# Giving up the unread TensorE products of a two-block model kernel (attention, mixers, routers, experts) on one Trainium2 core

## What is computed

```python
for layer in range(DEPTH):                      # first block
    z = rmsnorm(x, norm_mix[layer]) @ w_in[layer]
    x = x + concatenate([o_a, o_b, o_c, o_d]) @ w_out[layer]
    h = rmsnorm(x, norm_ffn[layer])
    x = x + (silu(h @ w_gate[layer]) * (h @ w_up[layer])) @ w_down[layer]
for i in range(DEPTH):                          # second block
    y = conformer_conv(h, ...) if i == 0 else short_gated_conv(h, ...)
    x = layer_norm(ALPHA * x + (1.0 + g_m) * y, ...)
    y = hierarchical_moe(h, ...)                # group, two experts a token
    x = layer_norm(ALPHA * x + (1.0 + g_f) * y, ...)
```

## The kernel before

| place | code | where | products |
|---|---|---|---|
| A | `ahead_of_scores(8)`, line 896 | between `values(8)` and `scores(10)`, in each layer's attention | 2, twice |
| B | line 2562 | between `conformer_in` and `normed_back(0)` (transposes, line 2475), ahead of `mix_out` (line 2507) | 3 |
| C | lines 2586 and 2599 | behind the router's products (line 2536) and behind the five small counting products (lines 2594 to 2598), in each expert layer | 4 and 1, twice |
| D | line 2884 | at the end of the first expert layer, ahead of `tile_transposes` (line 2393) and `gated_in` (line 2492) | 2 |

## Time and profile before

### The profile page before, as it was taken

One profiled execution on the slowest core, in us unless ns is written; L12 is line 12 of the kernel. 1 busy time (PEld: TensorE's weight loads), 2 busy tenths in 40 slices (PEclk: granted clock), 3 DMA queues, 4 the chain that ended last, 5 costly groups with the idle time before them and its releaser, 6 DMA issues.

```text
span 1958.8 us, 20949 instructions
## 1 busy us (share of the span) xinstructions
PE 1859.0 (95%) x8122; PEld 944.4 (48%) x8122; DVE 852.5 (44%) x1556; ACT 342.2 (17%) x800; POOL 93.0 (5%) x137
## 2 busy tenths in 40 slices
PE   8999999999999999999999999989999988989887
PEld 4555665456556654855343433433875323323222
DVE  1576888834778988864112111112325101111102
ACT  2453111124531102122011100101002100000000
POOL 4102000001020001201000000000000000000000
PEclk9999999999999999999999999999999999999999
DMA  9315877752168876666999999999448999999996
GB/s 308 106 60 175 307 286 266 256 186 56 60 232 290 296 293 227 185 251 233 420 425 430 432 431 431 432 430 409 161 188 335 428 430 431 430 431 432 430 429 281
DMA packets 138028, 603.18 MB, mean 308 GB/s; under 512 B 15864, under 2 KB 59816, under 8 KB 122560
## 3 DMA queue, kind: packets, MB, share of 16 engines
q1 hardware_dynamic: 131904, 591.41, 76.3%
q0 software_dynamic: 5136, 10.25, 2.0%
q10 hardware_dynamic: 880, 0.07, 0.0%
HBM read 597.70 MB, written 1.10 MB: 306 GB/s over the span
## 4 chain that ended last, share of the span: by engine, by line
PE 67%; DMA 22%; DVE 6%; DVEq 2%; issue 1%; ACT 1%; SPq 1%; ACTq 0%
PE ps L2706 15%; DMA ring<-in_e_w_gate 14%; PE ps L955 13%; PE ps L657 7%; DMA ring<-in_e_w_up 7%; PE ps L1038 5%; PE ps L2492 4%; PE ps L2742 4%; PE ps L2422 3%; PE ps L2507 2%; PE ps L2627 2%; PE ps L756 2%; PE ps L2605 2%; DMA ring<-in_e_w_down 1%; DMA ring<-in_b_w_in 1%
## 5 line engine op out<-in xcount | busy, mean ns | idle before, releaser
L2706 PE MATMUL ps<-ring,hT 128*64 128x512 f32 (+1 forms) x960 | 218.9, 609 | 28.8 <-DMA ring<-in_e_w_gate 17.6
L2706 PE MATMUL ps<-ring,late 128*64 128x512 f32 (+1 forms) x880 | 203.1, 606 | 24.8 <-DMA ring<-in_e_w_gate 14.5
L2742 PE MATMUL ps<-ring,qkT 128*64 128x512 f32 (+1 forms) x960 | 205.6, 594 | 2.8 <-DMA ring<-in_e_w_down 2.7
L657 PE MATMUL ps<-ring,hT 128*128 128x512 f32 (+1 forms) x384 | 171.0, 589 | 0.0
L2706 PEld LDWEIGHTS ps<-ring,hT 128*64 128x64 f32 (+1 forms) x960 | 68.6, 126 | 173.9 <-issue 173.9
L3375 DVE TENSOR_TENSOR qkT<-ps,qkT 128x512 f32<-128x512 f32 (+1 forms) x32 | 22.1, 690 | 279.5 <-PE ps L2706 277.1
L3351 DVE TENSOR_TENSOR qkT<-ps,qkT 128x512 f32<-128x512 f32 (+1 forms) x64 | 44.2, 690 | 218.1 <-PE ps L2742 218.0
L2706 PEld LDWEIGHTS ps<-ring,late 128*64 128x64 f32 (+1 forms) x880 | 64.7, 126 | 153.4 <-issue 153.3
L1680 DVE SCALAR_TENSOR_TENSOR qkT<-ring,cc,qkT 128x512 f32<-128x512 f32 x168 | 125.8, 749 | 8.2
L2742 PEld LDWEIGHTS ps<-ring,qkT 128*64 128x64 f32 (+1 forms) x960 | 61.1, 123 | 129.0 <-issue 128.6
L3370 DVE TENSOR_TENSOR x<-ps,x 128x1024 f32<-128x1024 f32 x22 | 26.9, 1224 | 194.4 <-PE ps L2605 194.4
(11 more groups left out here) (480 smaller groups left out, 2316.6 us busy)
## 6 DMA issues: line engine op xcount, KB each, us to landing
ring<-in_e_w_down SPq DMA_DIRECT2D x26, 4096.0 KB, 21.1
ring<-in_e_w_gate SPq DMA_DIRECT2D x26, 4096.0 KB, 21.8
ring<-in_e_w_up SPq DMA_DIRECT2D x24, 4096.0 KB, 21.8
ring<-in_ada_w SPq DMA_DIRECT2D x24, 2048.0 KB, 14.0
ring<-in_w_gate SPq DMA_DIRECT2D x16, 1408.0 KB, 8.2
ring<-in_w_up SPq DMA_DIRECT2D x16, 1408.0 KB, 8.5
ring<-in_w_down SPq DMA_DIRECT2D x22, 1024.0 KB, 5.0
ring<-in_e_w_gate SPq DMA_DIRECT2D x8, 2048.0 KB, 16.4
```

Source lines behind the costliest of these rows:

```text
L657: last = mm(m.ps[:, 4 + i, 0:chunk_width(n)], m.hT[:, j, i * P:(i + 1) * P], w[:, j, :], start=(j == 0), stop=(j == KC - 1))
L2706: last = mm(dst, xg[:, j, at + x * n_tok:at + x * n_tok + place], w(x, j), start=(j == 0), stop=(j == KC - 1))
L2742: lasts[x] = mm(dst, m.hidT[:, j, rows + x * place:rows + (x + 1) * place], half_of(w(x, j), n), start=(j == 0), stop=(j == 3))
```

## The change

All calls of the two helpers are given up. Nothing is put in their place and nothing else moves: the order of the remaining instructions, the waits and the transfers are the same. TensorE issues 19 products (38 records) fewer. The helpers' definitions stay, without a caller.

```diff
@@ -893,7 +893,7 @@
             if u == 2:
                 cmp_batch()
             elif u == 8:
-                unread(2)
+                pass
@@ -2559,7 +2559,6 @@
             conformer_in()
-            unread(3, 0)
             normed_back(0)
             mix_out(l, 0, 0)
@@ -2583,7 +2582,6 @@
         router(l, 0)
         router(l, 1)
-        unread(4, 5)
         if l == 1:
             pe.wait_ge(t["rel2"], 1)
@@ -2596,7 +2594,6 @@
         mm(m.ps[:, 7, 64:96], m.ones[:], m.A[:, 1, :], start=False, stop=True).then_inc(t["count_ps"], 1)
-        unread(1, 5)
         pe.wait_ge(t["zeros"], l + 1)
@@ -2881,7 +2878,7 @@
         if l == 0:
-            unread(2, 3)
+            pass
         if l == 0:
             pe.drain().then_inc(t["arrive2"], 1)
```

## The result

The changed kernel takes 1972.59 us (median of 4 runs, 1971.82 to 1975.71) against 1960.01 us before (4 runs). The ratio is 1.0071, 95% interval 1.0058 to 1.0083: 11 to 16 us slower. The forecast, 1965.8 us, had the right sign; the loss is twice the forecast 6 us and lies outside the range.

What follows compares the result with a forecast made beforehand. TensorE was taken as the bound, with weight transfers setting the pace inside expert stages. Terms 2.2 + 1.4 + 2.0 + 0.4 = +6.0 us gave 1966.7 us from the profiled execution, 1965.8 us adjusted to the median; range 1960.0 to 1969.6.

Steps and rivals of the forecast that it cites:

- the fifth at C: Unread product behind each router's counting products; not hidden, so its removal starts the gather 0.4 us earlier each time.
- C: Routers, two times: four products and a fifth go; clock falls, 1.4 us less 0.4 gained each, +2.0 us.
- A: Attention, two times: two products ahead of the scores, hidden by ScalarE; clock fall over transposes, 1.1 us each, +2.2 us.
- B: Ahead of the conformer's output product: three products hidden by VectorE; gap grows to 3.9 us, clock falls, +1.4 us.
- D: Between the expert layers: removal gives 0; about half a chance of a fall and half a stretch, +0.4 us.
- one fall costs 1.7 us: Price of a clock fall where TensorE is the bound: a burst of 8.78 us against 7.07 to 7.09 us.
- the discount for transposes: In attention, 1.1 us taken instead of a whole fall's 1.7 us, since mostly transposes would run low.
- the 0.4 us gained at each gather: At both routers: without the product behind the counting products, the gather starts 0.4 us earlier each time.
- Only long unbroken idle time counts: Rival: A and D keep the clock because short products break their gaps; +3.4 us, 1963.2 us; chance 0.17.
- The transfers swallow the delays: Rival: slack in the weight stream hides the delays of B and C; +2.6 us, 1962.4 us; chance 0.09.
- The clock holds: Rival: no fall anywhere, only the gather's 2 x 0.4 us are gained; 1959.0 us; chance 0.08.
- the products delay real work: Rival: at A and C removal frees real work and the clock holds; -5.4 us, 1954.4 us; chance 0.04.

Runs made afterwards that it cites:

- Without A: Kernel before with only the unread products in attention (two in each layer) given up; 1964.34 us against 1959.55 us, ratio 1.0028.
- without C: Kernel before with only the unread products behind each router and behind its counting products given up; 1965.13 us against 1959.55 us, ratio 1.0026.
- without B and D: Kernel before with only the unread products ahead of the conformer's output product and between the expert layers given up; 1963.28 us against 1959.55 us.
- changed kernel again: The changed kernel, unaltered, measured and profiled a second time against the kernel before; 1973.89 us against 1958.59 us, ratio 1.0068.

## Why the prediction was wrong in size

**Right.** The sign and the mechanism. None of the removed products but the fifth at C was ahead of ready work: the scores, the output product, the routing and `gated_in` are released by others as before. The clock fell at A, B, C and D, in every profile of a kernel in which the place was empty (three for each). The weight stream is not slack: its load went out at 928.81 us instead of 919.38 us, 9.4 us late, and `gated_in` behind all of the first mixture starts 9.8 us late (1386.35 against 1376.58 us). Without A, without C and without B and D the losses add up to the whole. The gaps' lengths (1.7, 3.8, and 4.3 us at the first router) are as forecast, within 0.2 us.

**Wrong: "one fall costs 1.7 us".** This is the step that failed. It took the single low stretch of the earlier trace rows as the price of a fall anywhere, and every upper bound of the sum was built on it or near it. The low stretches at the emptied places were often two or three times as long. What each place lost in the profiles, against the forecast, in us and worked out from starts as in the table above ("the part alone" is the kernel without A, without C, or without B and D):

| place | forecast | changed kernel | the part alone | changed kernel again |
|---|---|---|---|---|
| A, first and second | 1.1, 1.1 | 2.9, 1.6 | 1.3, 2.9 | 1.5, 1.3 |
| B | 1.4 | 1.5 | 2.9 | 2.9 |
| C, first and second | 1.0, 1.0 | 2.3, 1.6 | 2.8, 2.6 | 3.0, 1.7 |
| D | 0.4 | 1.7 | 2.0 | not parted from a wait for weights |

At the routers the stretch begins in the idle time, stays over the counting products and reaches through much of the gather, about 10 us, in both layers of all three profiles. At A it lies over the 16 transposes and is nearly 7 us long in two of six cases; at B in two of three, over wide products. So the terms were too small: A 2.2 us forecast, 4.8 us measured alone (upper bound of my sum 3.4); C 2.0 us net forecast, 5.6 us measured alone (upper bound 3.8). That B's 1.4 us agrees with the changed kernel's first profile is luck: the other two show twice as much. Why a stretch is short one time and long another at the same place stays open.

**Wrong: the discount for transposes.** A was given 1.1 us and not 1.7, since most of what would run low is transposes. The low clock costs them nearly their whole length too: 8 of them take 1.97 us at 0.50 and 1.07 us at 1.00. None of the six falls at A cost less than 1.3 us.

**Wrong: the 0.4 us gained at each gather.** I took the counting products' time from the earlier trace rows, at full clock. At 0.50 they come every 0.43 us, VectorE waits for them, and the gather starts 2.39 us behind the first of them (912.45 to 914.84) instead of 2.08. The gain exists only where the clock holds: 0.33 and 0.38 us with the fifth product alone given up.

**Too small: D.** Half a chance times half a stretch, 0.4 us, was a mean in a sum of likeliest values. In the profile the clock was at 0.50 in all of 1387 to 1390 us, over the first products of `gated_in`, 1.7 us, and it fell there in the other two profiles without D as well. Together with B it measures 3.7 us against 1.8 us.

**The rivals.** Only long unbroken idle time counts: excluded, since A fell in both layers of three profiles behind 1.69 us, while the burst at 1222.31 us in the earlier trace rows ran at full clock behind 2.63 us. The transfers swallow the delays: excluded by the load at 928.81 us. The clock holds, and the products delay real work: excluded at A by ScalarE's 130.74 us, at C by the routing.

What stays open is the exact share of chance. All the kernels have low stretches at places that the change does not touch, near 73, 459, 489, 780 and 1944 us and several times in the second mixture's experts, in some profiles and not in others. The one at 489 us costs 1.6 us in the changed kernel. The kernel before ranges from 1957 to 1964 us over 27 executions, and the profiled pair's 11.2 us is one draw of it.

## What to carry to other kernels

Idle time of TensorE that hides behind another engine is not free: ask what the clock does next and over which work. Don't take the price of one fall from one place: the same fall cost from 1.3 to 3.0 us here, and one profile of each kernel is not enough to size it. An unread product pays if it ends before the instruction that releases the next real work and if it works on all rows: at A, two cover the gap, four cost 3.6 us and none 4.8 us. It may also take the fall itself, as at the second router, where a low stretch over unread products cost about 0.4 us.

## What the runs showed of the hardware that was not expected

- Products that read 32 of 128 rows kept TensorE busy and left the clock at 0.50 (16.00 of 16 us at the first router), where the profile of before, with 128 rows, has 1.00. With this one difference at all the places the kernel is 19 us slower. It would fit the low stretch at 489 us, behind products of 32 and 18 rows with no idle time, but that one was not tried by itself.
- A low stretch can last far longer than the one at 1136 us: 6 us over wide products at B, about 10 us at both routers over nothing, counting products of 32 columns and the gather.
- Transposes and narrow products take nearly twice as long at the low clock: 8 transposes 1.97 us instead of 1.07, the counting products one every 0.43 us instead of every 0.22.
- Transposes in place of the products, occupying TensorE for about three quarters of the time, held the clock at A and B and not at the routers and D, and cost 6.0 us in all against 12.6 us for no filling.
